# Reordering the front of a transformer block: x tiles, projection weights and the last modulation quarters

## What is computed

```python
c_act = jax.nn.silu(c)
mod = (c_act @ w_ada + b_ada)                  # (1, 6*1024)
sh1, sc1, gt1, sh2, sc2, gt2 = jnp.split(mod, 6, axis=-1)
h = rmsnorm(x, g_mix) * (1.0 + sc1) + sh1
proj = h @ w_in                                # 448 columns for attention, 512 for pooling
y_mla = mla_mixer(proj[..., :448], positions, ...)    # latent attention, 4 heads
y_pool = pool_mixer(proj[..., 448:], w_pool, pool_scale)
x = x + gt1 * (concat(y_mla, y_pool) @ w_o)
h = rmsnorm(x, g_ffn) * (1.0 + sc2) + sh2
x = x + gt2 * ((silu(h @ w_gate) * (h @ w_up)) @ w_down)
return rmsnorm(x, g_final)
```

## Time and profile before

| | |
|---|---|
| median of 3 runs | 1142.1 us (1141.98 to 1143.61) |
| span of the profiled execution | 1139.2 us |
| TensorE busy | 1081.0 us, 95% |
| DVE busy | 560.2 us, 49% |
| ACT busy | 329.8 us, 29% |
| POOL busy | 197.5 us, 17% |
| DMA, mean over the span | 73 GB/s |

### The profile page before, as it was taken

One profiled execution on the slowest core, in us unless ns is written; L12 is line 12 of the kernel. 1 busy time (PEld: TensorE's weight loads), 2 busy tenths in 40 slices (PEclk: granted clock), 3 DMA queues, 4 the chain that ended last, 5 costly groups with the idle time before them and its releaser, 6 DMA issues.

```text
span 1139.2 us, 12752 instructions
## 1 busy us (share of the span) xinstructions
PE 1081.0 (95%) x5001; PEld 886.9 (78%) x5001; DVE 560.2 (49%) x906; ACT 329.8 (29%) x603; POOL 197.5 (17%) x176
## 2 busy tenths in 40 slices
PE   5799699999999999999999999999999999999994
PEld 1698477888877788888888888888888888888883
DVE  5849746766269876151422425052331515243257
ACT  1661166877211652110202011020301112020213
POOL 1223563041022311001010100101010010101224
PEclk9799899999999999999999999999999999999997
DMA  9803102002176034021212111021211202121103
GB/s 337 290 10 102 56 1 74 1 1 75 54 265 199 1 132 145 23 53 37 74 37 69 42 37 52 22 74 37 74 37 37 74 7 67 37 74 37 37 1 148
DMA packets 75365, 83.40 MB, mean 73 GB/s; under 512 B 3446, under 2 KB 54458, under 8 KB 75324
## 3 DMA queue, kind: packets, MB, share of 16 engines
q1 hardware_dynamic: 75324, 82.85, 22.6%
HBM read 78.65 MB, written 4.19 MB: 73 GB/s over the span
## 4 chain that ended last, share of the span: by engine, by line
PE 77%; DVE 10%; ACT 4%; issue 3%; POOL 3%; DMA 2%; SPq 2%; POOLq 0%; ACTq 0%; DVEq 0%
PE PS L1289 71%; PE PS L1463 2%; DMA ADA<-in_w_ada 2%; PE PS L1348 2%; DVE ACC L914 2%; DVE GT L914 2%; ACT HTf L789 1%; PE PS L1475 1%; POOL ropeQ L522 1%; ACT PR L712 1%; DVE WO1lo L926 1%; ACT PT L728 0%; POOL HT L554 0%; ACT HTf L601 0%; DVE PT L1109 0%
## 5 line engine op out<-in xcount | busy, mean ns | idle before, releaser
L1289 PE MATMUL PS<-HT,WGU 128*128 128x512 f32 x2112 | 482.9, 390 | 2.5 <-DVE WGU L1166 2.5
L1289 PEld LDWEIGHTS PS<-HT,WGU 128*128 128x128 f32 x2112 | 397.4, 188 | 85.9 <-issue 3.2
L1289 PE MATMUL PS<-WD,ACTS 128*128 128x512 f32 x1056 | 241.3, 389 | 0.4 <-DVE X L1265 0.4
L1289 PEld LDWEIGHTS PS<-WD,ACTS 128*128 128x128 f32 x1056 | 198.1, 188 | 42.0 <-DVE X L1265 0.9
L1206 DVE TENSOR_TENSOR HID<-HID,PS 128x512 f32<-128x512 f32 x44 | 30.2, 687 | 311.6 <-ACT HID L823 311.5
L823 ACT ACTIVATE HID<-PS 128x512 f32<-128x512 f32 x44 | 26.3, 598 | 487.7 <-PE PS L1289 487.7
L560 POOL TENSOR_TENSOR WDraw<-WDraw,GT 128x1024 f32<-128x1024 f32 x20 | 47.5, 2399 | 578.1 <-DMA WDraw<-in_w_down 547.4
L1225 DVE TENSOR_TENSOR X<-PS,X 128x512 f32<-128x512 f32 x160 | 108.5, 689 | 68.6 <-PE PS L1289 68.6
L1166 DVE TENSOR_TENSOR WGU<-WGUraw,WGU 128x2048 fp32r<-128x2048 f32 x22 | 51.2, 2329 | 6.2 <-ACT WGU L796 6.2
L796 ACT ACTIVATE WGU<-WGUraw 128x2048 fp32r<-128x2048 f32 x22 | 42.2, 1916 | 24.2 <-DMA WGUraw<-in_w_up 24.2
L1289 PE MATMUL PS<-HT,WU 128*128 128x512 f32 x192 | 46.0, 401 | 0.5 <-DVE WU L926 0.5
(11 more groups left out here) (191 smaller groups left out, 1170.4 us busy)
## 6 DMA issues: line engine op xcount, KB each, us to landing
ADA<-in_w_ada SPq DMA_DIRECT2D x20, 1024.0 KB, 6.0
WGUraw<-in_w_gate SPq DMA_DIRECT2D x22, 512.0 KB, 4.0
WGUraw<-in_w_up SPq DMA_DIRECT2D x22, 512.0 KB, 5.2
WDraw<-in_w_down SPq DMA_DIRECT2D x10, 1024.0 KB, 4.8
X<-in_x SPq DMA_DIRECT2D x16, 512.0 KB, 11.5
ADAS<-in_w_ada SPq DMA_DIRECT2D x4, 1024.0 KB, 9.1
out<-XG SPq DMA_DIRECT2D x8, 512.0 KB, 2.8
WUraw<-in_w_in SPq DMA_DIRECT2D x4, 512.0 KB, 9.5
```

The lines of the kernel that those rows point to most:

```text
L1289: ins = pe.matmul(ps, l, r, start=(n_ == 0), stop=(n_ == len(terms) - 1))
```

## The change

On SP, x(0), x(1) and the four projection weight pieces are issued earlier: the x tiles behind ada(0) and sh1(1), the weights behind ada(2), so that sh1(3) and ada(3) come after them. On ACT, the squares of x(1) come ahead of the copy of the sh1 row. On DVE, roots1(0) comes ahead of accumulate(1); the first two LO parts of the weights are made ahead of accumulate(3); after G1 come the other two, then h_lo(0) and only then roots1(2). On TensorE, turn_x1(0) and turn_x1(1) stand between the two halves of the sh1 sum. No computation is added or removed.

```diff
--- before.py
+++ after.py
@@ -310,17 +310,16 @@
         sp.dma_start(POSI[:], positions.rearrange("b (t p) -> p (b t)", p=P), allow_slow_non_contiguous=True).then_inc(S["pos_in"], 16)
         sp.dma_start(FREQ[:], freqs.partition_broadcast(P)).then_inc(S["freq_in"], 16)
         load_sh1(1)
+        load_x(0)
+        load_x(1)
         load_ada(1)
         load_sh1(2)
         load_ada(2)
-        load_sh1(3)
-        load_x(0)
-        load_ada(3)
-        for t in range(1, 4):
-            load_x(t)
         for i in range(4):
             sp.dma_start(WTMraw[:, 2 * i:2 * i + 2, :], win_d[:, 2 * i:2 * i + 2, 0:TM]).then_inc(wtm_in[i], 16)
-        for t in range(4, NT):
+        load_sh1(3)
+        load_ada(3)
+        for t in range(2, NT):
             load_x(t)
         sp.dma_start(GQ[:], g_q.rearrange("l n -> (l n)").partition_broadcast(P)).then_inc(S["gq_in"], 16)
         sp.dma_start(GKV[:], g_kv.rearrange("l n -> (l n)").partition_broadcast(P)).then_inc(S["gkv_in"], 16)
@@ -613,10 +612,11 @@
             act.wait_ge(S["tm_out"], t + 1)
 
         squares1(0)
+        squares1(1)
 
         act.wait_ge(S["sh1_rows"], 1)
         act.activation(SHROW[0:1], PS[0:1, 4:6, :], ACT.Copy).then_inc(S["sh1_out"], 1)
-        for t in range(1, 4):
+        for t in range(2, 4):
             squares1(t)
         for t in range(NT):
             modulate1(t)
@@ -942,11 +942,6 @@
                 then(ins)
         dve.sem_inc(S["ang_ready"], 1)
 
-        for j in range(1, 4):
-            accumulate(j)
-        dve.wait_ge(S["rowsT"], 1)
-        dve.tensor_copy(COLS[:], PS[:, 6, 0:N_ROWS])
-
         def roots1(t0):
 
             dve.wait_ge(S["ss1"], t0 + 2)
@@ -959,21 +954,29 @@
             dve.wait_ge(S["h_hi"], t + 1)
             lo(HT[:, LO, :, tok(t)], HTf[:, :, tok(t)], HT[:, HI, :, tok(t)], S["h_ready"])
 
+        def wtm_lo(i):
+            dve.wait_ge(S["wtm_hi"], i + 1)
+            lo(flat(WTM[:, LO, 2 * i:2 * i + 2, :]), flat(WTMraw[:, 2 * i:2 * i + 2, :]),
+               flat(WTM[:, HI, 2 * i:2 * i + 2, :]), S["wtm_ready"])
+
         roots1(0)
+        accumulate(1)
+        accumulate(2)
+        dve.wait_ge(S["rowsT"], 1)
+        dve.tensor_copy(COLS[:], PS[:, 6, 0:N_ROWS])
+        wtm_lo(0)
+        wtm_lo(1)
+        accumulate(3)
 
         dve.wait_ge(S["colsum"], 2)
         dve.wait_ge(S["sh1_sum"], 1)
         then(dve.tensor_tensor(MOD[:, 0:16], PS[:, 7, 0:16], COLS[:, 0:16], ALU.add))
         dve.scalar_tensor_tensor(G1[:], MOD[:, 8:16], 1.0, COLS[:, ROW_MIX:ROW_MIX + 8], ALU.add, ALU.mult).then_inc(S["modcols"], 1)
 
-        for i in range(4):
-            if i == 1:
-                roots1(2)
-            if i == 2:
-                h_lo(0)
-            dve.wait_ge(S["wtm_hi"], i + 1)
-            lo(flat(WTM[:, LO, 2 * i:2 * i + 2, :]), flat(WTMraw[:, 2 * i:2 * i + 2, :]),
-               flat(WTM[:, HI, 2 * i:2 * i + 2, :]), S["wtm_ready"])
+        wtm_lo(2)
+        wtm_lo(3)
+        h_lo(0)
+        roots1(2)
         for t in range(1, NT):
             h_lo(t)
             if t in (1, 3):
@@ -1308,8 +1311,20 @@
 
         pe.wait_ge(S["rows_in"], 64)
         pe.transpose(PS[:, 6, 0:N_ROWS], ROWS[0:N_ROWS, :], IDENT[0:N_ROWS, 0:N_ROWS]).then_inc(S["rowsT"], 1)
+        def turn_x1(t):
+
+            pe.wait_ge(S["xn1"], t + 1)
+            if t >= 2:
+                pe.wait_ge(S["hmod"], t - 1)
+            for k in range(KT):
+                ins = pe.transpose(PS[:, 2 * (t % 2) + k // 4, (k % 4) * P:(k % 4 + 1) * P], X[:, t, k * P:(k + 1) * P], IDENT[:])
+            ins.then_inc(S["t1"], 1)
+
         pe.wait_ge(S["act_silu"], 1)
         for ch in range(2):
+            if ch == 1:
+                turn_x1(0)
+                turn_x1(1)
             for t in range(KT):
                 if t % 4 == 0:
                     pe.wait_ge(sh1_in[2 * ch + t // 4], 16)
@@ -1323,18 +1338,6 @@
         ins.then_inc(S["sh1_sum"], 1)
         col_sum(1)
 
-        def turn_x1(t):
-
-            pe.wait_ge(S["xn1"], t + 1)
-            if t >= 2:
-                pe.wait_ge(S["hmod"], t - 1)
-            for k in range(KT):
-                ins = pe.transpose(PS[:, 2 * (t % 2) + k // 4, (k % 4) * P:(k % 4 + 1) * P], X[:, t, k * P:(k + 1) * P], IDENT[:])
-            ins.then_inc(S["t1"], 1)
-
-
-        turn_x1(0)
-        turn_x1(1)
         for t in range(NT):
             if t < NT - 2:
                 turn_x1(t + 2)
```

## The result

| | before | changed |
|---|---|---|
| median | 1142.4 us (6 runs, 1140.9 to 1143.6) | 1148.9 us (6 runs, 1146.4 to 1151.8) |
| ratio to before | | 1.0058, 95% interval 1.0044 to 1.0071 |
| span of the profiled execution | 1139.2 us | 1147.3 us |
| end of G1 | 38.35 us | 42.73 us |
| first projection matmul | 45.91 us | 53.71 us |

The kernel became slower by 0.58%, about 6.6 us (6.4 by the medians); 9.0 were forecast, and 1148.9 lies in the range. The two profiled executions differ by 8.1 us, of which 7.7 are there when the gate column sums start.

The account below looks back on a forecast made before the run. The first projection matmul's time (45.91 us) was taken as the bound, passed on fully to the end. G1 5.6 us later plus 3.4 behind it gave 9.0: span 1148.2, median 1151.1 us, range 1146.8 to 1154.5.

Parts of the forecast that it names:

- Rival (1): Not slower: TensorE's wait before the gate column sums swallows the shift; 1142.1 us, or 1144 with part absorbed; chance 0.05.
- the 9.4 us wait: TensorE's longest wait after 46 us, before the gate column sums, for DVE's accumulations; forecast to stay some 9 us long.
- part 1: Loads: 2.36 MB move ahead of ada(3), 6.05 us at 390 GB/s; ada(3) lands at 34.5, first weight piece at 25.6.
- rival (4): Loads do not come in that order, so DVE waits at roots1(0) for x(1) or weights; chance 0.02.
- part 2: DVE up to accumulate(3): roots end at 26.7, xn1 at 27.8 and 29.2, accumulate(3) at 40.8 (bounds 38.9 to 41.1).
- part 3: TensorE up to G1: idle until 27.9, transposes 3.67, second sh1 half 7.7; G1 at 44.0, 5.6 us later.
- Rival (2): A milder shift: xn1 meets no rounding, sh1 records run at the high clock; 5.5 us, 1147.6; chance of 1144.4 to 1147 0.07.
- Rival (3): The sh1 sums stay at the low clock; first matmul 13 to 17 us late, 1155 to 1159 us; chance 0.10.
- M: The end of G1: 38.35 us before, forecast at 44.0 in the changed kernel.
- part 4: G1 to first projection matmul: 11.0 us instead of 7.56, 3.4 more, as roots1(2) is queued behind h_lo(0)'s wait.

Follow-up runs that it names:

- c_front_busy: c_front with ten added matmuls, results unused, in TensorE's gaps (five awaiting sh1(3), four ahead of turn_x1(2), one behind); ratio to before 0.9975.
- a_loads_back: The changed kernel with the load order of before, the engines' order as changed; ratio to before 1.0121, in a second round 1.0133.
- b_loads_alone: The kernel before with only the changed order of the loads on SP; ratio to before 1.0072.
- a_busy_gap: The changed kernel with seven added matmuls, results unused, in TensorE's gap between the first sh1 half and turn_x1(0); ratio to before 1.0063.
- b_roots_behind: The kernel before with only roots1(2) moved behind all four wtm_lo and h_lo(0); ratio to before 1.0034.
- a_roots_first: The changed kernel with roots1(2) right behind G1, ahead of wtm_lo(2), wtm_lo(3) and h_lo(0); ratio to before 1.0043.
- b_busy: The kernel before with two added matmuls of 512 columns, results unused, between turn_x1(1) and turn_x1(2); ratio to before 0.9990.
- c_front: The kernel before with x(0), x(1) loaded ahead of sh1(3), weights still behind ada(3), and ACT's and DVE's front reordered; ratio to before 0.9988.
- a_turns_late: The changed kernel with turn_x1(0) and turn_x1(1) back behind col_sum(1), loads and DVE as changed; ratio to before 1.0067.

## Why the prediction was right, and where its steps were off

**The bound.** "A later first projection matmul should be a later end, microsecond for microsecond" held: 7.8 us at the first matmul, 7.6 where tile 0 ends, 7.7 at the gate sums, 8.1 over the span. More exactly it is the end of tile 0, not its start, that is passed on, since the tile's own length changes with the clock: in all ten changed or edited kernels with an undisturbed trace the gate sums start as much later or earlier as tile 0 ends, within 0.1 us (from 2.6 earlier in c_front_busy to 15.7 later in a_loads_back). Rival (1) fell: the 9.4 us wait was found again in full, since all of DVE's queue had moved with it.

**The loads (part 1)** landed as worked out. POOL's wait for the first weight piece ended at 25.91 (25.6 forecast), and the loads alone delayed DVE's start on ada(3) by 6.6 us (6.05 forecast); rival (4) fell. That this alone costs as much as the whole change I had not said: by my words "no longer the transfer, is late". That is so in the changed kernel, where DVE fills the time until ada(3) with the early roots, but b_loads_alone shows the loads as enough of a cause.

**DVE ahead of the sum (part 2).** Idle from 20.1 to 23.2 and roots from there, as forecast. The roots were not held by a rounding (25.91 came 0.3 us behind them), and the two xn1 took 2.10 (1.42 without a rounding beside them), so they were done at 27.6 and not at 29.2. What was held instead is accumulate(1): 4.87 us for 3.11. Three of its four instructions took 1.30 to 1.41 us, the last 0.75, and the roundings beside them 1.37 where one alone takes 0.94. I had priced the exclusion for the roots and xn1 and carried the accumulate at 3.1. The Trainium skill, "SBUF — State Buffer", section "Who interferes with whom", names every DVE instruction with two SBUF inputs, and an accumulate is one. The trace agrees with 1.76 us, and a_loads_back has it again (4.86). The two errors cancelled: accumulate(3) ended at 40.6, 40.8 forecast.

**TensorE ahead of the sum (part 3)** is where the size was off. The gap, the transposes at 3.67 and the second half as one block are there, but the block began at 30.0 and not at 31.6, because xn1(0) was done at 26.4 and not at 27.8. It took 8.1 us from start to start (8.16 by its row), 7.7 forecast. The clock:

```profile
22.00:23.00 1.00, 0.00 (x0) 0.00 (x0) 0.00 (x0) 0.97 (x2) 0.00 (x0) 0.54 1.04 383
...
32.00:33.00 1.00, 1.00 (x3) 0.17 (x2) 0.96 (x2) 0.00 (x0) 0.00 (x0) 0.84 1.08 399
```

It went from 2.4 to 1.2 GHz at 22.1, 2.2 us after the last record, and came back 5.9 us after the first transpose, two records into the block as I had taken it, or one more. G1 at 42.7 instead of 44.0 is the sum: a block that began 1.6 early (roots done at 25.6 instead of 26.7, 0.9 of it the hold that did not occur, and a first xn1 of 0.8 instead of 1.1), took 0.4 longer, and 0.1 less behind it. This 1.3 is the term of the sum that was mis-sized, and it takes the forecast of 9.0 to 7.7, what the traces show within 0.1. That accumulate(3) came as forecast, by the two errors that cancelled, was luck; G1 did not hang on it, since TensorE's last sum began 0.6 us after it ended. Rival (2) was right in one half of a part: the roots went ahead of the first rounding, but the second xn1 met it (1.43 us for 0.75), and the sh1 records did not all run at the high clock. Rival (3) fell. a_busy_gap shows that less waiting on TensorE's side would have brought at most the 0.6 us to DVE.

**From M to the first matmul (part 4)**: 10.98 us, 11.0 forecast, and by its steps: h_lo(0) at M + 4.2, a root instruction held for 1.02 by POOL's rounding of tile 1, xn1(2) at M + 9.3. Only the transposes were 1.62 from start to start, not 1.97: the length of a row includes a modelled end. b_roots_behind prices this step alone at 3.4 to 3.9 us, 3.4 forecast. a_roots_first gives 3.4 of it back at the first matmul of the changed kernel, but 2.0 where tile 0 ends, since the tile then meets the low clock for longer.

**The span and the median.** I put 2.9 us around the span, the difference to the median. In the changed kernel the profiled execution took 1149.07 with a span of 1147.3, 1.8 us around. By the same 1.8 the profiled execution of before was one of its faster ones, 1141.0, against a median of 1142.4. This is why the traces differ by 8.1 us and the medians by 6.4. The interval of the ratio is 5.0 to 8.1 us; the traces' difference is at its very end. Such a scatter goes with the clock: of the 46 executions of the kernel before that ran beside the experiments, the three with a mean granted clock of 0.976 took 1144.8 to 1145.5 us, the five with 0.982 took 1139.5 to 1140.4. In the front this is seen in single rows. The first 16 sh1 records took from 8.4 us (b_busy) to 9.9 (a_busy_gap) in kernels whose loads and TensorE program are equal up to there, and the column sum behind accumulate(3) took 1.75 us in the kernel before and 1.05 in b_busy, equal up to there as a whole. Where else in an execution the clock differs from run to run is not shown, since no kernel has two undisturbed traces.

**Not settled.** The experiments say what each part costs under one order of the others; the sum of the parts is not the change, since the loads (8 us alone) and the engines' order (14 us alone) are 6.6 us together. The kernel was not tried with the weights behind ada(3) and everything else as changed.

## What to carry to other kernels

Before moving a load ahead of the one on which a chain hangs, count its bytes at the queue's rate: 2.36 MB were 6 us here, and the new order on the engines won hardly any of it back. Count them for each load that now comes later: in c_front half a megabyte ahead of ada(3) was a whole one ahead of sh1(3), and MOD waited for the chain behind sh1(3). Before moving a step behind a wait, ask what covered it: roots1(2) was free beside ACT and POOL's work on tile 0 and cost 3.4 us behind it. And a gap on TensorE has a second price at its end, in the clock, so a change that lets it idle before dense work should be costed with the rows of the low level.

## What the runs showed of the hardware

Ten executions of nearly the same front show the first projection tile of 24 matmuls at 5.13 us with the clock up and at 5.8 to 7.85 us else, according to when in it the clock rose; in c_front it rose 6.0 us after the first matmul, in the kernel before 3.0 us after it. With TensorE idle, it fell 2.2 us after the last record in the changed kernel, 3.7 in c_front and 5.0 in a_turns_late. With matmuls of 512 columns in TensorE's gaps the ratio fell by 0.1% (b_busy) and, from c_front to c_front_busy, by 0.13%, neither clear of the intervals; in the traces tile 0 ended 1.1 and 2.9 us earlier. A column sum of 8 records took 1.05 us at the high level and 1.86 at the low one. DVE's accumulate, four instructions, lost 1.76 us beside the last three of POOL's four roundings, where the two xn1 lost 0.7 beside the first and one root instruction of the kernel before 0.74.
